# Two block layers on one core: the last two norms' roots on GpSimd, one sigmoid table, ten spare products

## The reference, cut to what matters

```python
    x = x + _hier_moe(_rmsnorm(x, norm_ffn_g), ...)          # 32 experts, 2 per token
    hp = _rmsnorm(x, norm_ple_g)
    x = x + (p @ w_ple) * jax.nn.sigmoid(hp @ w_ple_gate)    # p: 256 x 256, w_ple_gate: 1024 x 1024
    return _rmsnorm(x, final_norm_g)

def _rmsnorm(x, g):
    r = lax.rsqrt(jnp.mean(x * x, axis=-1, keepdims=True) + EPS)      # EPS = 1e-6
    return x * r * g
```

## Time and profile before

| | |
|---|---|
| median of 3 runs | 698.94 us (695.62 to 700.0) |
| profiled execution: its own time | 697.35 us |
| its span, first to last instruction | 695.4 us |
| TensorE busy | 639.1 us (92%) |
| VectorE busy | 380.4 us (55%) |
| ScalarE busy | 283.6 us (41%) |
| GpSimd busy | 52.3 us (8%) |
| HBM traffic | 251 GB/s over the span |

### The profile page before, as it was taken

The page is one execution under the profiler, slowest core; times in us unless marked ns, Lnnn a source line. Parts: engine busy times, 40 slices in busy tenths (PEclk is TensorE's granted clock), DMA queues, the critical chain, the costliest instruction groups (busy, mean ns, idle before and its releaser), DMA issues.

```text
span 695.4 us, 11069 instructions
## 1 busy us (share of the span) xinstructions
PE 639.1 (92%) x4338; PEld 481.7 (69%) x4342; DVE 380.4 (55%) x670; ACT 283.6 (41%) x440; POOL 52.3 (8%) x74
## 2 busy tenths in 40 slices
PE   7999999899999999999999999899999857688693
PEld 4999997799999999995796888544444422224263
DVE  6686964768776666675776464522222220203375
ACT  6764363565555555546846721401111000010366
POOL 1000000300000000003094600000000000000000
PEclk9999999999999999999999999999999997989997
DMA  9944541737755555105804249999899999999901
GB/s 325 345 137 159 204 148 44 271 128 241 235 191 188 190 183 181 61 0 210 290 1 134 109 142 431 419 433 422 341 429 429 426 427 427 426 428 426 394 17 60
DMA packets 54488, 174.75 MB, mean 251 GB/s; under 512 B 4662, under 2 KB 29362, under 8 KB 48050
## 3 DMA queue, kind: packets, MB, share of 16 engines
q1 hardware_dynamic: 53776, 172.54, 64.7%
q10 hardware_dynamic: 674, 1.69, 0.7%
HBM read 173.17 MB, written 1.05 MB: 251 GB/s over the span
## 4 chain that ended last, share of the span: by engine, by line
PE 72%; DMA 13%; DVE 7%; ACT 5%; issue 1%; another core or an unknown queue 1%; SPq 0%; DVEq 0%; ACTq 0%
PE ps L1764 15%; PE ps L1766 15%; PE ps L1765 15%; DMA arena<-in_w_moe_dram 12%; PE ps L2279 6%; PE ps L2263 4%; PE ps L2336 4%; PE ps L2285 2%; PE ps L1961 2%; PE ps L2019 1%; DVE wpg_low L1689 1%; PE ps L2109 1%; PE ps L2060 1%; DMA x_tok<-in_x_dram 1%
## 5 line engine op out<-in xcount | busy, mean ns | idle before, releaser
L1764 PE MATMUL ps<-hT_high,w_up_high 128*128 128x256 f32 x352 | 99.7, 283 | 0.9 <-DVE w_up_low L1257 0.9
L1765 PE MATMUL ps<-hT_low,w_up_high 128*128 128x256 f32 x352 | 99.6, 283 | 0.0
L1766 PE MATMUL ps<-hT_high,w_up_low 128*128 128x256 f32 x352 | 99.6, 283 | 0.0
L1764 PEld LDWEIGHTS ps<-hT_high,w_up_high 128*128 128x128 f32 x352 | 67.5, 192 | 1.7 <-DVE w_up_low L1257 1.4
L1765 PEld LDWEIGHTS ps<-hT_low,w_up_high 128*128 128x128 f32 x352 | 67.5, 192 | 0.4
L1766 PEld LDWEIGHTS ps<-hT_high,w_up_low 128*128 128x128 f32 x352 | 67.5, 192 | 0.0
L1257 DVE TENSOR_TENSOR w_up_low<-W,w_up_high 128x1024 fp32r<-128x1024 f32 x44 | 52.8, 1227 | 24.0 <-ACT w_up_high L789 24.0
L789 ACT CAST w_up_high<-W 128x1024 fp32r<-128x1024 f32 x44 | 44.6, 1047 | 28.7 <-PE ps L1766 28.7
L952 ACT ACTIVATE sg<-ps 128x256 f32<-128x256 f32 x9 | 3.5, 384 | 123.3 <-PE ps L2279 123.3
L1764 PE MATMUL ps<-h_high,dense_high 128*128 128x256 f32 x160 | 45.7, 286 | 0.0
L2279 PE MATMUL ps<-W,junk 128*32 128x512 f32 x304 | 37.1, 617 | 9.1 <-DMA W<-in_w_moe_dram 9.0
(11 more groups left out here) (479 smaller groups left out, 1364.0 us busy)
## 6 DMA issues: line engine op xcount, KB each, us to landing
W<-in_w_moe_dram SPq DMA_DIRECT2D x25, 2048.0 KB, 21.2
arena<-in_w_moe_dram SPq DMA_DIRECT2D x19, 2048.0 KB, 26.5
W<-in_w_up_dram SPq DMA_DIRECT2D x22, 1024.0 KB, 8.8
W<-in_w_in_dram SPq DMA_DIRECT2D x8, 2048.0 KB, 11.0
W<-in_w_down_dram SPq DMA_DIRECT2D x11, 1024.0 KB, 5.1
hh<-in_w_moe_dram SPq DMA_DIRECT2D x4, 2048.0 KB, 30.0
W<-in_w_out_dram SPq DMA_DIRECT2D x2, 2048.0 KB, 8.9
W<-in_w_o_dram SPq DMA_DIRECT2D x2, 2048.0 KB, 8.5
```

The costliest lines, as they stand in the source:

```text
L1764: pe.matmul(o, lhs[0], rhs[0], start=first, stop=False, skip_group_check=True)
L1765: pe.matmul(o, lhs[0], rhs[1], start=False, stop=False, skip_group_check=True)
L1766: return pe.matmul(o, lhs[1], rhs[0], start=False, stop=last_k, skip_group_check=True)
```

## The change

1. ScalarE takes the squares of `norm(4)` in `squares_ple` without the root. GpSimd adds `EPS` and raises to the power -0.5, for both blocks.
2. The final norm: VectorE adds the two sums and `EPS` in one instruction; GpSimd raises the sum to the power -0.5; `root` and both reciprocals go. `scaled` and VectorE's scaling wait for GpSimd.
3. One activation that brings in the sigmoid table stands behind the fourth rounded piece of the gate weight; the other switches and their small activations are gone.
4. In the last group, in front of the wait for the second down piece, TensorE issues ten products of 128 x 512 on `Yp` into bank 1. Nothing reads them.

```diff
+        minus_half = stat[:, 61:62]
 # gpsimd, at its end
+            pool.wait_ge(sig("step_clear"), 2)
+            pool.memset(minus_half, -0.5).then_inc(sig("step_clear"), 1)
+            pool.wait_ge(sig("step_clear"), 3)
+            for b in range(TB):
+                pool.wait_ge(sig("std_ready"), 2 * 4 + b + 1)
+                pool.tensor_scalar(stat[:, 16 + b:17 + b], stat[:, 16 + b:17 + b], EPS, None, ALU.add).then_inc(sig("step_clear"), 1)
+                pool.wait_ge(sig("step_clear"), 4 + b)
+                pool.tensor_tensor(stat[:, 18 + b:19 + b], stat[:, 16 + b:17 + b], minus_half, ALU.pow).then_inc(sig("rple_ready"), 1)
+            for b in range(TB):
+                pool.wait_ge(sig("sum_ready"), b + 1)
+                pool.tensor_tensor(stat[:, 22 + b:23 + b], small[:, 38 + b:39 + b], minus_half, ALU.pow).then_inc(sig("ms_ready"), 1)
 # scalar
-            def root(b):
-                act.wait_ge(sig("ms_ready"), 2 * b + 1)
-                act.activation(stat[:, 22 + b:23 + b], small[:, 38 + b:39 + b], ACT.Sqrt,
-                               bias=epsc[:]).then_inc(sig("fstd_ready"), 1)
+            def squares_ple(b):
+                act.wait_ge(sig("x_ready"), 2 * 3 + b + 1)
+                act.activation((junk[:], hn[:, 0, :])[b], x_tok[:, b, :], ACT.Square, scale=D ** -0.5,
+                               accum_out=stat[:, 16 + b:17 + b]).then_inc(sig("std_ready"), 1)
             def scaled(b, half):
-                act.wait_ge(sig("ms_ready"), 2 * b + 2)
+                act.wait_ge(sig("ms_ready"), b + 1)
             round_gate((2, 3))
+            act.activation(small[:, 42:43], epsc[:], ACT.Sigmoid).then_inc(sig("table_ready"), 1)
             round_hp((2, 3))
             round_hp((0, 1))
             round_gate((4, 5))
-            norm(4)
+            squares_ple(0)
+            squares_ple(1)
             round_gate((6, 7))
-            act.activation(small[:, 42:43], epsc[:], ACT.Sigmoid).then_inc(sig("table_ready"), 1)
             gated(0, 0)
             gated(0, 1)
             squared(0, 0)
             squared(0, 1)
             gated(1, 0)
-            act.activation(small[:, 43:44], epsc[:], ACT.Sqrt).then_inc(sig("table_ready"), 1)
             squared(1, 0)
-            root(0)
-            act.activation(small[:, 44:45], epsc[:], ACT.Sigmoid).then_inc(sig("table_ready"), 1)
             scaled(0, 1)
             gated(1, 1)
-            act.activation(small[:, 42:43], epsc[:], ACT.Sqrt).then_inc(sig("table_ready"), 1)
             squared(1, 1)
-            root(1)
             scaled(1, 1)
 # vector
             lower_gate((6, 7))
-            for b in range(TB):
-                dve.wait_ge(sig("std_ready"), 2 * 4 + b + 1)
-                dve.reciprocal(stat[:, 18 + b:19 + b], stat[:, 18 + b:19 + b]).then_inc(sig("rple_ready"), 1)
...
-                        dve.tensor_tensor(small[:, 38 + b:39 + b], small[:, 34 + 2 * b:35 + 2 * b], small[:, 35 + 2 * b:36 + 2 * b],
-                                          ALU.add).then_inc(sig("ms_ready"), 1)
-                        dve.wait_ge(sig("fstd_ready"), b + 1)
-                        dve.reciprocal(stat[:, 22 + b:23 + b], stat[:, 22 + b:23 + b]).then_inc(sig("ms_ready"), 1)
-                        dve.wait_ge(sig("ms_ready"), 2 * b + 2)
+                        dve.scalar_tensor_tensor(small[:, 38 + b:39 + b], small[:, 34 + 2 * b:35 + 2 * b], EPS, small[:, 35 + 2 * b:36 + 2 * b],
+                                                 ALU.add, ALU.add).then_inc(sig("sum_ready"), 1)
+                        dve.wait_ge(sig("ms_ready"), b + 1)
 # tensor, in expert_down
             for f in range(DNC):
+                if g == NGRP8 - 1 and f == DNC - 1:
+                    for _ in range(10):
+                        pe.matmul(ps[:, 1, :], Yp[:, 1, 0:P], Yp[:, 0, :], start=True, stop=True, skip_group_check=True)
                 landed_chunk(item(CPG * g + UPC + f))
```

## The result

| | before | changed |
|---|---|---|
| median | 697.75 us (6 runs, 695.62 to 700.0) | 693.48 us (6 runs, 692.83 to 695.9) |
| ratio to before | | 0.9946, 95% interval 0.9925 to 0.9967 |
| profiled execution's span | 695.4 us | 690.8 us |

The change makes the kernel 0.5% faster; 694.6 us and a span of 691.1 were forecast. With three more runs the median of the kernel before came down by 1.2 us, from 698.94 to 697.75.

What follows compares the result with a forecast made beforehand. The weight stream bounds the time up to the last landings, then the engine chain behind it; gains of 3.36, 0.66, 0.15 and 0.16 us, together 4.33, took the median from 698.94 to 694.6 us, range 692.0 to 697.6.

Steps and rivals of the forecast that it cites:

- Step 1: Last down piece: spare products keep TensorE's clock up, saving 1.5 us, of which 0.66 arrives because gate weight's landing stays.
- The clock rival: TensorE's clock not kept up, or falling later, in gaps before the gate product: costs 1.5 us; chance 13%.
- Step 2: ScalarE before the gate: first sigmoid at 673.6, not 677.48; TensorE ends at 683.95, 0.66 and 0.15 us earlier.
- Step 3: VectorE's work on the third part: third sigmoid follows a square ending at 679.35; block 0's sum is ready at 682.5.
- Step 4: Final norm: the power on GpSimd takes 0.4 us from VectorE's sum to scaling, where root and reciprocal took 0.56.
- X: Final norm, time from the end of VectorE's sum to the start of scaling: 0.4 us, bounds 0.15 and 1.2.
- The slack of block 0: Block 0's scaling ahead of the fourth sigmoid: the power's price is free there up to 0.83 us.
- The sum: Whole gain: 3.36 waiting for ScalarE, 0.66 clock, 0.15 TensorE's stumble, 0.16 root and reciprocal, together 4.33 us.
- A dear first power: GpSimd's first power, for block 0's gate norm: free up to 4.3 us; one of 6.2 costs 1.9; chance 6%.
- Each power dear: Every GpSimd power far dearer than small rows: break-even at 2.8 us, at 5 us 4.45 slower; chance 5%.
- Switches left over: ScalarE: table switches remain if squares or roundings are not in the sigmoid's table; given no chance.

Runs made afterwards that it cites:

- no_spare_again: The changed kernel without its ten spare products: median 694.32 us, ratio 0.9954 to the kernel before.
- spare_only: The kernel before with the ten spare products and nothing else of the change: median 696.86 us, ratio 0.9993.
- the second set: Follow-up runs on one chip, the kernel before and the unaltered changed kernel measured again: medians 698.61 us and 693.10 us.
- late_only: The changed kernel with only its final norm part kept; `norm(4)` as before, no spare products: median 696.50 us, ratio 0.9975 to the kernel before.
- vector_order: The changed kernel with VectorE's turned halves ahead of rests of gate weight pieces in the gate stage: median 691.85 us, ratio 0.9910 to the kernel before.
- vector_order_again: The kernel of vector_order, unaltered, measured again on another set's chip: median 691.50 us, ratio 0.9910 to the kernel before.
- vector_plain: The kernel of vector_order without the ten spare products: median 693.05 us, ratio 0.9937 to the kernel before.

## Why the prediction was right, step by step

**Step 1, the spare products: the size held in the two profiles compared, the reason only in part.** From 1.70 us behind L the first rest moved to 1.08: 0.62 for 0.66. That the landing eats the rest of the 1.5 us is shown by the 0.78 us wait. But "the clock falls ahead of the last down piece, and the products prevent it" describes one kind of execution. The profile of before happened to be of that kind; in others the fall came in the gate product and cost 1.7, or not at all, and in `no_spare_again` a fall ahead of the down piece cost 2.0. That the 0.66 came out in the profile of the change is in part luck. The clock rival, given 13%, named the right place, the gaps ahead of the gate product, and nearly the price (1.5 for 1.7); with ten products it came true in one profile, of `spare_only`, and in none of the changed kernel's two. What the products are worth over many executions is about 1 us by the medians, and 1.5 in the new order on VectorE, with overlapping intervals.

**Step 2, ScalarE up to the first sigmoid.** It starts at L + 16.7 after L + 20.9: 4.2 earlier, where 3.9 were forecast against a fixed L. TensorE ends at L + 27.4 after L + 28.17, 0.77 for the forecast 0.81. On the table switch the measurement stands against the 2.66 us of the Trainium skill (page "ScalarE: Activation LUTs", section "What ACT_TABLE_LOAD costs"): the activation behind the one load left starts 1.30 us after the load does, as before.

**Step 3** put the third sigmoid at 679.35 and block 0's sum at 682.5; with L 0.79 earlier they would be 678.56 and 681.7, and are 678.22 and 681.43.

**Step 4, the power: the term that was mis-sized.** X was put at 0.4 and is 0.66, of which the power itself is 0.55. It is inside the bounds of 0.15 and 1.2, but above root and reciprocal together (0.56), so this term is a loss of 0.1 and not a gain of 0.16. The gain comes from the switches that the powers make unnecessary. The estimate took twice VectorE's time for an addition, 0.16. For an addition that is not far off: GpSimd's of one element took 0.21 to 0.30 us. The power took 0.55, and it also reads two operands where this addition reads one; which of the two makes it dearer no run separates. The slack of block 0 was 0.57 us behind an X of 0.66, so 1.23 in all against the 0.83 reckoned.

**The sum.** 3.36 + 0.66 + 0.15 + 0.16 = 4.33 forecast; measured from L: 4.03 gained at the fourth sigmoid (L + 31.53 to L + 27.50, of which 0.77 are TensorE's earlier end and 3.26 the wait on ScalarE), less 0.10 for X and less 0.09 for a store that took longer: 3.8. So the sum is half a microsecond too large: 0.26 of it is X, 0.1 the gap between TensorE's end and the fourth sigmoid, 0.09 the store. The medians differ by 4.27, and that this meets 4.3 to a tenth is luck: the same two kernels differ by 5.5 in the second set (698.61 and 693.10), and the interval of the ratio is 3 us wide.

**The rivals.** A dear first power: it took 0.87 us, in GpSimd's first work after 229 us of idling, against 0.55 later, and was hidden. Being the first doesn't explain the 0.3 us: in `late_only` GpSimd's first power took 0.56 after 246 us of idling, with VectorE idle.

```profile
686.07 0.56 POOL L653 TENSOR_TENSOR stat<-small,stat 128x1 f32<-128x1 f32 x1 [245.71 <-DVE small L1718]
```

The 6 us that the Trainium skill (page "GPSIMD Engine Reference", section "Instruction dispatch") gives for a freshly loaded kernel show nowhere. Each power dear: X is 0.66, far from 2.8. Switches left over: one load in the stage, as its order said.

## What to carry to other kernels

Ask of each table switch what the engine behind it waits for: in the profiles the two in front of the first sigmoid (one gone, one moved into idle time) were worth more than the three behind it, because everything later inherits their delay. Moving a tiny operation to an idle engine pays for what it frees, not for itself. When a clock's fall shows in one profile, take several before pricing it, and compare them from a common landing; and after an edit look for the wait that took the old one's place, here VectorE's on the rounding of piece 0, worth another 1.2 us.

## What the runs showed of the hardware

GpSimd's one-element instructions were slower while VectorE streamed. In the changed kernel the additions took 0.30 and 0.21 us, and the powers 0.87 beside VectorE's `lower_hp` (669.98 to 671.27) and 0.56 where VectorE was idle at the start and took up `lower_gate` (at 671.68) on the way. In `vector_order` VectorE runs without a gap from 662.47 to 675, on instructions with two inputs in SBUF:

```profile
667.20 1.19 POOL L653 TENSOR_SCALAR stat<-stat 128x1 f32<-128x1 f32 x1 [227.69 <-ACT junk L1019]
668.47 0.87 POOL L655 TENSOR_TENSOR stat<-stat 128x1 f32<-128x1 f32 x1
669.42 1.30 POOL L653 TENSOR_SCALAR stat<-stat 128x1 f32<-128x1 f32 x1
670.80 1.40 POOL L655 TENSOR_TENSOR stat<-stat 128x1 f32<-128x1 f32 x1
672.23 0.69 ACT L1005 ACTIVATE W<-ps,stat 128x512 f32<-128x512 f32 x1 [1.69 <-POOL stat L655]
```

An addition of one element took 1.19 and 1.30 us, about the length of one of VectorE's instructions on 1024 elements (1.2), and the second sigmoid waited 1.69 us for the power. It cost nothing, as VectorE reached that part only at 673.87. `vector_order_again` and `vector_plain` show the same four lengths within 0.01 us. The first power takes 0.87 here too, so not every instruction stretches further in the stream. The final powers, taken while VectorE waits, are 0.55 or 0.56 in every kernel. The Trainium skill (page "GPSIMD Engine Reference", section "Specifications") says that the two engines share SBUF interfaces and contend where VectorE has two SBUF inputs; these rows agree. That the shared interface is the cause was not tested by itself.
